# Differential attention: split scores, combination by a ratio, norm spread over the heads, on one Trainium2 core

## The chip, the cores and the metric

The kernel runs on one core of a Trainium2 chip. The metric is the device time of one execution in microseconds (us), lower is better. The kernel before took 3026.08 us, the median of three runs from 3018.17 to 3027.29 us.

## What is computed

Two transformer blocks over 512 tokens of width 1024 in float32; the change touches one sublayer of the second, the differential attention:

```
q, k, v = split(h @ w_qkv, 3)                 # 8 heads, two halves of 64 each in q and k, v of 128
q, k = rope on the first 16 of each 64;  q = q * 64 ** -0.5
p = softmax(q k^T)                            # for each head and each half c = 0, 1
a = p[:, :, 0] - lam_full * p[:, :, 1]
o = a @ v
o = rms_norm(o, subln_g) * (1 - lam_init)     # over the 128 of a head
return o.reshape(b, s, d) @ w_o
```

## The kernel before

The five engines are written out by hand: each has one list of instructions in program order (the blocks `sync`, `gpsimd`, `scalar`, `vector` and `tensor`), and they meet only through counting semaphores. An instruction that waits holds everything behind it on its engine. SP loads the weights (512 KB a unit) into four slots of `stage`. For every weight unit ScalarE writes a rounded copy `w_hi` (`hi`, L611), VectorE the remainder `w_lo` (`lo`, L1030), in rings of two; TensorE takes three products of half-width float32 (fp32r) for one of float32: hi by hi, lo by hi, hi by lo (`product`, L1706 to L1708), 24 matmuls a unit of 128 output columns.

The stage `qkv` has 24 such units: v in the first 8, then k, then q. VectorE copies each result out of PSUM into `raw` (L1612). For k and q, POOL issues four small DMAs that swap rows into `turned_raw` (L593), and one unit later VectorE turns the tile by three operations (L1620, L1622, L1626) into `k_t` or `q_t`. TensorE waits for all 16 tiles (`roped`, 48) before the first score.

The heads are 32 tiles m, four query tiles of 128 tokens to each of 8 heads. A tile passes: scores of both halves, 64 rows each, in float32 (L2269, TensorE, PSUM banks 0 to 3 in two pairs); maxima (L1641, VectorE); two exponentials with their sums (L984, ScalarE); reciprocal, scaling of half 1, combination (L1647, L1649, L1652, VectorE); four transposes (L2278, TensorE); copy into `PT` (L993, ScalarE); product with v (L2257, TensorE). The exponentials have two buffers, `E`. A finished head is copied to `o_raw` (`take_o`, L1634).

Only when all heads are done does the norm of o begin: squares (L1000), their sums by one-column matmuls (L2288), one root (L1002), reciprocal, then per head a broadcast copy `rexp` (L1665), its transposes (L2296), the scaling (L1672), the rounded copy `h_hi` (L1006) and the remainder `h_lo` (L1678). TensorE waits for the last `h_lo`, and then takes the 8 units of `w_o` (`attn_out`), L1706 to L1708 again, each followed by the addition to x.

## Time and profile before

| | us |
|---|---|
| three runs: lowest, median, highest | 3018.17, 3026.08, 3027.29 |
| profiled execution: its own time | 3019.3 |
| its span, first to last instruction | 3017.6 |
| mean granted TensorE clock | 0.964 of full |

Times in the rows count from the start of the span. PE is TensorE's matmuls, PEld its weight loads, DVE VectorE, ACT ScalarE, POOL GpSimd. A float32 matmul stands as two records, an fp32r one as one. The stretch in question runs from the last qkv unit, which ends at 2455.7 (its copy out of PSUM starts at 2455.74), to the start of the third unit of `w_o` at 2596.7.

### The profile page before, as it was taken

To read this page: it belongs to the slowest core of one execution; us is meant where nothing else is said; L and a number is where in the kernel's file an instruction comes from. 1 tells how busy PE (TensorE), PEld (TensorE's weight loads), DVE (VectorE), ACT (ScalarE), POOL (GpSimd) and SP (SyncE) were. 2 spreads that over 40 slices of the span, in tenths; PEclk is the share of its full clock that TensorE was granted. 3 is DMA by queue.
4 is the path that set the end of the run, shared out by engine and by line. 5 is a ranking of instruction groups with operands and counts; after the bars stand their busy time and mean duration, and the time that the engine had idled before them with its cause. 6 is when DMAs were issued, how large, how long until landed. Compare 5 with 4: busy or idle time off the path is not lost.

```text
span 3017.6 us, 40643 instructions
## 1 busy us (share of the span) xinstructions
PE 2874.0 (95%) x16133; PEld 2300.3 (76%) x16133; DVE 1456.7 (48%) x2079; ACT 977.1 (32%) x1548; POOL 233.1 (8%) x310
## 2 busy tenths in 40 slices
PE   7989978899999999999979999999999989899998
PEld 6844767788888787888868888788887854788887
DVE  4355655366677655555463332333323478433322
ACT  3234234333333223222233222322223236332222
POOL 1000010011100011001110000100001120100000
PEclk9769989999999999999979999999999999899999
DMA  5100500066322364555412223222232220122232
GB/s 216 69 1 1 180 24 3 3 219 227 116 94 96 113 201 153 195 195 190 149 53 91 97 93 93 87 98 97 96 96 95 97 71 1 56 91 97 96 91 71
DMA packets 91955, 310.20 MB, mean 103 GB/s; under 512 B 11824, under 2 KB 15664, under 8 KB 91696
## 3 DMA queue, kind: packets, MB, share of 16 engines
q1 hardware_dynamic: 69040, 231.77, 22.8%
q0 software_dynamic: 22784, 76.56, 7.6%
q8 instruction: 97, 1.59, 0.2%
q14 instruction: 34, 0.28, 0.0%
HBM read 305.14 MB, written 2.10 MB: 102 GB/s over the span
## 4 chain that ended last, share of the span: by engine, by line
PE 88%; DVE 7%; ACT 2%; issue 1%; DMA 0%; POOL 0%; SPq 0%; DVEq 0%; ACTq 0%
PE psum L1706 24%; PE psum L1708 24%; PE psum L1707 24%; PE psum L1931 1%; PE psum L1919 1%; PE psum L1871 1%; PE psum L1721 1%; PE psum L1781 1%; DVE nmax L1641 1%; PE psum L1777 1%; PE psum L1778 1%; PE psum L2269 1%; PE psum L2037 1%; PE psum L2092 1%; PE psum L1943 1%
## 5 line engine op out<-in xcount | busy, mean ns | idle before, releaser
L1030 DVE TENSOR_TENSOR w_lo<-stage,w_hi 128x1024 fp32r<-128x1024 f32 (+3 forms) x445 | 519.6, 1168 | 849.0 <-ACT w_hi L611 846.8
L1706 PE MATMUL psum<-h_hi,w_hi 128*128 128x512 f32 x2248 | 882.5, 393 | 12.2 <-POOL h_lo L578 8.3
L1707 PE MATMUL psum<-h_lo,w_hi 128*128 128x512 f32 x2248 | 879.4, 391 | 0.0
L1708 PE MATMUL psum<-h_hi,w_lo 128*128 128x512 f32 x2248 | 879.3, 391 | 0.0
L611 ACT ACTIVATE w_hi<-stage 128x1024 fp32r<-128x1024 f32 (+3 forms) x445 | 450.3, 1012 | 1267.8 <-PE psum L1708 1237.0
L1706 PEld LDWEIGHTS psum<-h_hi,w_hi 128*128 128x128 f32 x2248 | 424.1, 189 | 105.1 <-POOL h_lo L578 8.7
L1708 PEld LDWEIGHTS psum<-h_hi,w_lo 128*128 128x128 f32 x2248 | 424.0, 189 | 90.1
L1707 PEld LDWEIGHTS psum<-h_lo,w_hi 128*128 128x128 f32 x2248 | 424.2, 189 | 87.9
L1706 PE MATMUL psum<-hid_hi,w_hi 128*128 128x512 f32 x880 | 343.0, 390 | 6.5 <-DVE hid L1115 6.5
L1707 PE MATMUL psum<-hid_lo,w_hi 128*128 128x512 f32 x880 | 342.4, 389 | 0.0
L1708 PE MATMUL psum<-hid_hi,w_lo 128*128 128x512 f32 x880 | 342.4, 389 | 0.0
L1706 PEld LDWEIGHTS psum<-hid_hi,w_hi 128*128 128x128 f32 x880 | 165.2, 188 | 42.7 <-DVE hid L1115 8.7
L1707 PEld LDWEIGHTS psum<-hid_lo,w_hi 128*128 128x128 f32 x880 | 165.2, 188 | 34.4
L1708 PEld LDWEIGHTS psum<-hid_hi,w_lo 128*128 128x128 f32 x880 | 165.2, 188 | 34.3
L1115 DVE TENSOR_TENSOR hid<-s_buf,psum 128x512 f32<-128x512 f32 x88 | 60.5, 688 | 266.5 <-PE psum L1708 264.8
L1066 DVE CUSTOM_DVE_ANT_0 mod_w<-mod_w,c_act 128x1024 f32<-128x1024 f32 x144 | 175.6, 1219 | 0.0
L498 POOL DMA_DIRECT2D mod_w<-in_mod_w x144 | 76.9, 534 | 1125.7 <-DVE modv L1066 948.4
L668 ACT ACTIVATE hid_hi<-hid 128x512 f32 (+1 forms) x110 | 67.9, 618 | 56.0 <-DVE hid L1115 56.0
L622 ACT ACTIVATE norm_t<-xT 128x512 f32<-128x512 f32 x64 | 40.3, 630 | 131.9 <-DVE xT L1139 121.6
L519 POOL TENSOR_TENSOR rexp<-norm_t 128x512 f32<-128x512 f32 x7 | 9.0, 1286 | 945.2 <-ACT norm_t L622 945.2
L1122 DVE TENSOR_TENSOR hid_lo<-hid,hid_hi 128x512 f32 (+1 forms) x110 | 75.3, 685 | 0.0
L519 POOL TENSOR_TENSOR rexp<-rexp,norm_t 128x512 f32<-128x512 f32 x35 | 45.1, 1288 | 268.4 <-ACT norm_t L622 268.4
(397 smaller groups left out, 2744.8 us busy)
## 6 DMA issues: line engine op xcount, KB each, us to landing
stage<-in_up SPq DMA_DIRECT2D x220, 512.0 KB, 3.2
mod_w<-in_mod_w POOLq DMA_DIRECT2D x144, 512.0 KB, 4.1
stage<-in_down SPq DMA_DIRECT2D x80, 448.0 KB, 3.3
stage<-in_down SPq DMA_DIRECT2D x40, 512.0 KB, 3.5
stage<-in_w_in SPq DMA_DIRECT2D x24, 512.0 KB, 4.3
stage<-in_w_qkv SPq DMA_DIRECT2D x24, 512.0 KB, 3.2
stage<-in_w_merge SPq DMA_DIRECT2D x16, 512.0 KB, 4.5
PTn<-in_cmp_w SPq DMA_DIRECT2D x1, 4096.0 KB, 12.0
```

The costliest lines, as they stand in the source:

```text
L498: pool.dma_start(mod_w[:, slot], A["mod_w"][bass.ds(t, 1)].rearrange("a p n -> (a p) n")).then_inc(mod_in[slot], 16)
L519: pool.tensor_tensor(sq_sum, sq(n_norm, 0) if k == 1 else sq_sum, sq(n_norm, k), ALU.add).then_inc(acc_done, 1)
L611: act.activation(w_hi[:, c % 2, 0:kt * cols], stage[:, c % NSTAGE, 0:kt * cols], ACT.Copy).then_inc(hi_done, 1)
L622: act.activation(sq(n_norm, k), xT[:, k], ACT.Square).then_inc(sq_done, 1)
L668: act.activation(hid_hi[:, bass.ds(2 * i + q, 1), :].rearrange("p a n -> p (a n)"), hid[:, q], ACT.Copy).then_inc(hidhi_done, 1)
L1030: dve.tensor_tensor(w_lo[:, c % 2, 0:kt * cols], stage[:, c % NSTAGE, 0:kt * cols], w_hi[:, c % 2, 0:kt * cols].bitcast(F32), ALU.subtract ...
L1066: dve.tensor_tensor_reduce(out=mod_w[:, t % 2], in0=mod_w[:, t % 2], in1=c_act[:], scale=1.0, scalar=0.0, op0=ALU.mult, op1=ALU.add, accum ...
L1115: dve.tensor_tensor(hid[:, q], s_buf[:, q], taps[:, 1] if f == 0 else bank(s.tile + 2 * q + 1), ALU.mult).then_inc(hid_done, 1)
L1122: dve.tensor_tensor(hid_lo[:, tile, :].rearrange("p a n -> p (a n)"), hid[:, q], hid_hi[:, tile, :].rearrange("p a n -> p (a n)").bitcast( ...
L1706: pe.matmul(dst, wh[:, n], a_hi[:, k], start=start and n == 0, stop=False)
L1707: pe.matmul(dst, wh[:, n], a_lo[:, k], start=False, stop=False)
L1708: m = pe.matmul(dst, wl[:, n], a_hi[:, k], start=False, stop=stop and n == kt - 1)
```

## The change

1. k and q are split like weights: ScalarE rounds the turned tile (`qk_round`), VectorE writes the remainder (`qk_low`), and a score is three fp32r products per half (`score`) in place of one float32 product. Scores of a head wait for its own tiles, the first one for `raw_done`; the turning of the last two q tiles and three remainders are moved behind the first maxima, with the `lo` of the second unit of `w_o`.
2. Combination by a ratio: the scaling of half 1 over 512 columns goes; a ratio of one column is formed, and half 0 takes half 1 times the ratio. The common factor that is left goes into the norm, whose eps is multiplied by the square of the sum of half 0 (`var_o`).
3. `E` gets a third buffer; the transposes lag three tiles and use one bank; ScalarE copies the turned tile to `PT` ahead of the exponentials of its tile. `E` lies in `mod_w` and `c_act`, `o_raw` in `v_tok`, and `rope`, `raw`, `turned_raw` in `PT`.
4. Square, sum and variance of a head are moved between the tiles (`SQUARE_AT`, `SUM_AT`, `VAR_AT`). The root is taken in two parts; the spread is a matmul of `orstd` (no `rexp`), and the first two units of `w_o` are taken part by part as the heads get ready (`first_out`). POOL writes `h_lo` of the odd heads.

The core of the diff; "..." marks what is left out, the removed lines of the old functions for the most part:

```diff
+def by_token(x):
+    return x.rearrange("p (t n) -> p t n", t=TT)
+ROOTS = ((0, 5), (5, 8))
+SQUARE_AT = {4 * h + 12: h for h in range(6)}
+SUM_AT = {4 * h + 13: h for h in range(6)}
+VAR_AT = {4 * h + 14: h for h in range(5)}
...
-        q_t, k_t, v_tok, rope, raw, E, PT, o_raw, turned_raw = phase(
-            ("q_t", [P, KD, S], F32), ("k_t", [P, KD, S], F32), ("v_tok", [P, TT, D], F32), ("rope", [P, 2, S], F32),
-            ("raw", [P, 2, S], F32), ("E", [P, 2, 2, S], F32), ("PT", [P, 2, TT, S], F32), ("o_raw", [P, DIFF_HEADS, S], F32),
-            ("turned_raw", [P, 2, S], F32))
+        qk_hi, qk_lo, v_tok, PT, es, ovar = phase(
+            ("qk_hi", [P, 2 * KD, S], F32R), ("qk_lo", [P, 2 * KD, S], F32R), ("v_tok", [P, TT, D], F32),
+            ("PT", [P, 2, TT, S], F32), ("es", [P, DIFF_HEADS * TT, 2], F32), ("ovar", [P, DIFF_HEADS * TT], F32))
+        rope, raw, turned_raw = PT[:, 0, 0:2], PT[:, 1, 0:2], PT[:, 1, 2:4]
+        k_hi, q_hi, k_lo, q_lo = qk_hi[:, 0:KD], qk_hi[:, KD:], qk_lo[:, 0:KD], qk_lo[:, KD:]
+        spare = c_act[:].rearrange("p (a s) -> p a s", a=2)
+        E = [mod_w[:, n].rearrange("p (c s) -> p c s", c=2) for n in range(2)] + [spare]
+        o_sq = [norm_t[:, h % 2] for h in range(6)] + [spare[:, 0], spare[:, 1]]
+        o_raw = [v_tok[:, :, h * P:(h + 1) * P] for h in range(DIFF_HEADS)]
...
+for h in range(1, DIFF_HEADS, 2):
+    pool.wait_ge(ohi_done, h + 1)
+    pool.tensor_tensor(h_lo[:, h], turn_t[h % 4], h_hi[:, h].bitcast(F32), ALU.subtract).then_inc(olo_pool, 1)
...
+    def qk_round(m):
+        act.wait_ge(roped, 3 * (m - 7))
+        act.activation(qk_hi[:, m - 8], norm_t[:, m % 2], ACT.Copy).then_inc(qkhi_done, 1)
+    for n in range(23):
         hi(s.first + n + 2)
...
+        if n >= 10:
+            qk_round(n - 2)
...
+    def root_o(n):
+        first, last = ROOTS[n]
+        act.wait_ge(ovar_done, last)
+        act.activation(ostd[:, TT * first:TT * last], ovar[:, TT * first:TT * last], ACT.Sqrt,
+                       scale=float(D // P)).then_inc(ostd_done, 1)
+    def round_o(h):
+        act.wait_ge(ot_done, h + 1)
+        act.activation(h_hi[:, h], turn_t[h % 4], ACT.Copy).then_inc(ohi_done, 1)
...
+    for m in range(4 * DIFF_HEADS + 3):
+        if m >= 3:
+            g = m - 3
             h, j = g // 4, g % 4
             act.wait_ge(a_turned, g + 1)
+            if g == 0:
+                act.wait_ge(roped, 48)
             if h >= 2 and j == 0:
                 act.wait_ge(pv_done, h - 1)
             act.activation(PT[:, h % 2, :, j * P:(j + 1) * P],
-                           psum[:, 4 + g % 2, :].rearrange("p (t n) -> p t n", t=TT),
+                           psum[:, 4, :].rearrange("p (t n) -> p t n", t=TT),
                            ACT.Copy).then_inc(pt_done, 1)
...
+        if m < 4 * DIFF_HEADS:
+            act.wait_ge(max_done, m + 1)
+            for c in range(2):
+                act.activation(E[m % 3][:, c], psum[:, 2 - 2 * (m % 2) + c, :], ACT.Exp,
+                               bias=nmax[:, m % 2, c:c + 1],
+                               accum_out=es[:, m, c:c + 1]).then_inc(exp_done, 1)
+        if m == 0:
+            hi(s.first + 25)
+        if m < 3:
+            qk_round(21 + m)
+        if m in SQUARE_AT:
+            square_o(SQUARE_AT[m])
+    for step, h in (("sq", 6), ("root", 0), ("sq", 7), ("hi", 0), ("hi", 1), ("root", 1), ("hi", 2), ("hi", 3),
+                    ("hi", 4), ("hi", 5), ("hi", 6), ("hi", 7)):
+        {"sq": square_o, "hi": round_o, "root": root_o}[step](h)
...
+    def qk_low(m):
+        dve.wait_ge(qkhi_done, m - 7)
+        dve.tensor_tensor(qk_lo[:, m - 8], norm_t[:, m % 2], qk_hi[:, m - 8].bitcast(F32),
+                          ALU.subtract).then_inc(qklo_done, 1)
...
+    for n in range(24):
+        dve.wait_ge(unit_done, s.first + n + 1)
+        if n >= 10:
+            dve.wait_ge(roped, 3 * (n - 9))
+        dve.tensor_copy(raw[:, n % 2], bank(s.tile + n)).then_inc(raw_done, 1)
+        if n == 23:
+            continue
+        lo(s.first + n + 2)
+        if n >= 10:
+            qk_low(n - 2)
         if n >= 9:
+            turn_qk(n - 1)
...
+    def var_o(h):
+        cols = slice(TT * h, TT * h + TT)
+        dve.wait_ge(exp_done, 2 * TT * (h + 1))
+        dve.scalar_tensor_tensor(out=ovar[:, cols], in0=es[:, cols, 0], scalar=EPS * P / D, in1=es[:, cols, 0],
+                                 op0=ALU.mult, op1=ALU.mult).then_inc(ovar_step, 1)
+        dve.wait_ge(ovar_step, h + 1)
+        dve.wait_ge(ossq_done, h + 1)
+        dve.tensor_tensor(ovar[:, cols], ovar[:, cols], psum[:, 5, cols], ALU.add).then_inc(ovar_done, 1)
+    def rec_o(n):
+        cols = slice(TT * ROOTS[n][0], TT * ROOTS[n][1])
+        dve.wait_ge(ostd_done, n + 1)
+        dve.reciprocal(orstd[:, cols], ostd[:, cols]).then_inc(orstd_done, 1)
+    def norm_o(h):
+        if h >= 4:
+            if h % 2:
+                dve.wait_ge(olo_pool, h // 2 - 1)
+            else:
+                dve.wait_ge(olo_done, h // 2 - 1)
+        dve.wait_ge(obc_done, h + 1)
+        dve.scalar_tensor_tensor(out=by_token(turn_t[h % 4]), in0=o_raw[h], scalar=sub_gain[:, 0:1],
+                                 in1=by_token(psum[:, 3 * (h % 2), :]), op0=ALU.mult, op1=ALU.mult).then_inc(ot_done, 1)
+    def low_o(h):
+        dve.wait_ge(ohi_done, h + 1)
+        dve.tensor_tensor(h_lo[:, h], turn_t[h % 4], h_hi[:, h].bitcast(F32), ALU.subtract).then_inc(olo_done, 1)
...
-            dve.tensor_reduce(nmax[:, m % 2], psum[:, 2 * (m % 2):2 * (m % 2) + 2, :], AX.X, ALU.max,
+            dve.tensor_reduce(nmax[:, m % 2], psum[:, 2 - 2 * (m % 2):4 - 2 * (m % 2), :], AX.X, ALU.max,
                               negate=True).then_inc(max_done, 1)
+        if m == 0:
+            lo(s.first + 25)
+            qk_low(21)
         if 1 <= m <= M:
             g = m - 1
             b = g % 2
             dve.wait_ge(exp_done, 2 * g + 2)
-            dve.reciprocal(coef[:, b], esum[:, b]).then_inc(comb_step, 1)
-            dve.wait_ge(comb_step, steps + 1)
-            dve.tensor_scalar(E[:, b, 1], E[:, b, 1], coef[:, b, 1:2], neg_lam[:, 0:1], ALU.mult,
+            dve.reciprocal(coef[:, b, 1:2], es[:, g, 1:2]).then_inc(comb_step, 1)
+            dve.wait_ge(comb_step, 3 * g + 1)
+            dve.tensor_scalar(coef[:, b, 0:1], es[:, g, 0:1], coef[:, b, 1:2], neg_lam[:, 0:1], ALU.mult,
                               ALU.mult).then_inc(comb_step, 1)
...
+            dve.wait_ge(comb_step, 3 * g + 2)
+            dve.scalar_tensor_tensor(out=E[g % 3][:, 0], in0=E[g % 3][:, 1], scalar=coef[:, b, 0:1],
+                                     in1=E[g % 3][:, 0], op0=ALU.mult, op1=ALU.add).then_inc(comb_step, 1)
+        if 2 <= m <= 3:
+            qk_low(20 + m)
+        if 1 <= m <= 2:
+            turn_qk(21 + m)
+        if m >= 11 and (m - 11) % 4 == 0:
+            take_o((m - 11) // 4)
+        if m in VAR_AT:
+            var_o(VAR_AT[m])
+    for step, h in (("var", 5), ("take", 6), ("rec", 0), ("take", 7), ("norm", 0), ("var", 6), ("norm", 1), ("low", 0),
+                    ("var", 7), ("norm", 2), ("rec", 1), ("norm", 3), ("low", 2), ("norm", 4), ("low", 4),
+                    ("norm", 5), ("norm", 6), ("low", 6), ("norm", 7)):
+        {"take": take_o, "rec": rec_o, "norm": norm_o, "var": var_o, "low": low_o}[step](h)
...
+    def score(m):
+        h, cols = m // 4, slice(m % 4 * P, m % 4 * P + P)
+        pe.wait_ge(qklo_done, 9 + h)
+        if m == 0:
+            pe.wait_ge(raw_done, 23)
+        if m == 1:
+            pe.wait_ge(raw_done, 24)
+        for n, (q, k) in enumerate(((q_hi, k_hi), (q_lo, k_hi), (q_hi, k_lo))):
+            for c in range(2):
+                rows = slice(HD * c, HD * c + HD)
+                last = pe.matmul(psum[:, 2 - 2 * (m % 2) + c, :], q[rows, h, cols], k[rows, h, :],
+                                 start=n == 0, stop=n == 2)
+        last.then_inc(score_done, 1)
...
+    def sum_o(h):
         pe.wait_ge(osq_done, h + 1)
+        if h >= 1:
+            pe.wait_ge(ovar_done, h)
         for tt in range(TT):
+            last = pe.matmul(psum[:, 5, TT * h + tt:TT * h + tt + 1], o_sq[h][:, tt * P:(tt + 1) * P],
                              means[:, 0:1], start=True, stop=True)
         last.then_inc(ossq_done, 1)
...
+    def spread_o(h):
+        pe.wait_ge(orstd_done, 1 if h < ROOTS[0][1] else 2)
         if h >= 2:
             pe.wait_ge(ot_done, h - 1)
         for tt in range(TT):
+            at = TT * h + tt
+            last = pe.matmul(psum[:, 3 * (h % 2), tt * P:(tt + 1) * P],
+                             orstd[:, at:at + 1].to_broadcast([P, P]), ident, start=True, stop=True)
         last.then_inc(obc_done, 1)
+    def first_out(k):
+        s = seg["attn_out"]
+        kt, cols = shape_of(s.first)
+        pe.wait_ge(ohi_done, k + 1)
+        for e in range(2):
+            c = s.first + e
+            if k == 0:
+                pe.wait_ge(lo_done, c + 1)
+            wh, wl, dst = slot(w_hi, c, kt, cols, 2), slot(w_lo, c, kt, cols, 2), bank(s.tile + e)
+            pe.matmul(dst, wh[:, k], h_hi[:, k], start=k == 0, stop=False)
+            pe.matmul(dst, wl[:, k], h_hi[:, k], start=False, stop=False)
+            if k % 2:
+                pe.wait_ge(olo_pool, k // 2 + 1)
+            else:
+                pe.wait_ge(olo_done, k // 2 + 1)
+            last = pe.matmul(dst, wh[:, k], h_lo[:, k], start=False, stop=k == KD - 1)
+            if k == KD - 1:
+                last.then_inc(unit_done, 1)
...
+    for m in range(M + 3):
+        if m < M:
+            if m >= 2:
+                pe.wait_ge(exp_done, 2 * (m - 1))
+            score(m)
+        if m >= 3:
+            g = m - 3
+            pe.wait_ge(comb_step, 3 * (g + 1))
+            if g >= 1:
+                pe.wait_ge(pt_done, g)
+            for kt in range(TT):
+                last = pe.transpose(psum[:, 4, kt * P:(kt + 1) * P],
+                                    E[g % 3][:, 0, kt * P:(kt + 1) * P], ident)
+            last.then_inc(a_turned, 1)
+        if m >= 7:
+            weigh((m - 7) // 4, (m - 7) % 4)
+        if m in SUM_AT:
+            sum_o(SUM_AT[m])
+    for kt in range(TT):
+        weigh(DIFF_HEADS - 1, kt)
+    for step, h in (("sum", 6), ("spread", 0), ("spread", 1), ("sum", 7), ("out", 0), ("spread", 2), ("out", 1),
+                    ("spread", 3), ("out", 2), ("spread", 4), ("out", 3), ("spread", 5), ("out", 4),
+                    ("spread", 6), ("out", 5), ("spread", 7), ("out", 6), ("out", 7)):
+        {"sum": sum_o, "spread": spread_o, "out": first_out}[step](h)
+    def out_unit(n):
+        if n >= 2:
+            product(seg["attn_out"].first + n, 0, range(KD), (h_hi, h_lo), seg["attn_out"].tile + n, True, True)
+    mixed_out("attn_out", 7, out_unit)
```

VectorE (DVE), from the last copy out of PSUM to the first combination. Before:

```order
L1612 COPY raw<-psum 128x512 [waits roped,unit_done]
L1030 TENSOR_TENSOR w_lo<-stage,w_hi 128x1024 [waits hi_done]
L1620 SCALAR_TENSOR_TENSOR q_t<-turned_raw,rope 128x512 [waits raw_done,swapped0]
L1622 SCALAR_TENSOR_TENSOR raw<-raw,rope 128x512
L1626 TENSOR_TENSOR q_t<-q_t,raw 128x512 [waits roped]
L1620 SCALAR_TENSOR_TENSOR q_t<-turned_raw,rope 128x512 [waits raw_done,swapped1]
...
L1641 TENSOR_REDUCE nmax<-psum 128x2 [waits score_done] x2
L1647 RECIPROCAL coef<-esum 128x2 [waits exp_done]
L1649 TENSOR_SCALAR E<-E,coef,neg_lam 128x512 [waits comb_step]
L1652 SCALAR_TENSOR_TENSOR E<-E,coef 128x512 [waits comb_step]
```

Now (`PT` stands for `raw`, `mod_w` for `E`):

```order
L1672 COPY PT<-psum 128x512 [waits roped,unit_done]
L1720 TENSOR_REDUCE nmax<-psum 128x2 [waits score_done]
L1072 TENSOR_TENSOR w_lo<-stage,w_hi 128x1024 [waits hi_done]
L1651 TENSOR_TENSOR qk_lo<-norm_t,qk_hi 128x512 [waits qkhi_done]
L1720 TENSOR_REDUCE nmax<-psum 128x2 [waits score_done]
L1729 RECIPROCAL coef<-es 128x1 [waits exp_done]
L1731 TENSOR_SCALAR coef<-es,coef,neg_lam 128x1 [waits comb_step]
L1734 SCALAR_TENSOR_TENSOR mod_w<-mod_w,coef 128x512 [waits comb_step]
L1661 SCALAR_TENSOR_TENSOR norm_t<-PT 128x512 [waits raw_done,swapped0,qklo_done]
L1663 SCALAR_TENSOR_TENSOR PT<-PT 128x512
L1666 TENSOR_TENSOR norm_t<-norm_t,PT 128x512 [waits roped]
```

The maxima of tile 0 stand ahead of the second `w_o` remainder, and the turnings come after combinations.

TensorE, from the last product with v to the first products with `w_o`. Before (of eight groups of sums and eight of transposes one each is shown):

```order
L2257 MATMUL psum<-PT,v_tok 128x512 x3
L2288 MATMUL psum<-cst,norm_t 128x1 [waits osq_done]
L2288 MATMUL psum<-cst,norm_t 128x1 x3
...
L2296 MATMUL psum<-cst,rexp 128x128 [waits ot_done,orexp_done]
L2296 MATMUL psum<-cst,rexp 128x128 x3
L1706 MATMUL psum<-h_hi,w_hi 128x512 [waits lo_done,olo_done]
```

Now:

```order
L2338 MATMUL psum<-PT,v_tok 128x512 x3
L2348 MATMUL psum<-cst,c_act 128x1 [waits ovar_done,osq_done]
...
L2358 MATMUL psum<-cst,orstd 128x128 [waits orstd_done]
...
L2371 MATMUL psum<-h_hi,w_hi 128x512 [waits lo_done,ohi_done]
L2372 MATMUL psum<-h_hi,w_lo 128x512
L2377 MATMUL psum<-h_lo,w_hi 128x512 [waits olo_done]
...
L2358 MATMUL psum<-cst,orstd 128x128 [waits ot_done,orstd_done]
L2358 MATMUL psum<-cst,orstd 128x128 x3
L2371 MATMUL psum<-h_hi,w_hi 128x512 [waits ohi_done]
```

Two groups of sums are left there, and products with `w_o` stand between the spreads.

## Rows read from the trace of the kernel before

**Rows 1.** The page, part 4: chain that ended last, shares by engine.
```profile
PE 88%; DVE 7%; ACT 2%; issue 1%; DMA 0%; POOL 0%; SPq 0%; DVEq 0%; ACTq 0%
```

**Rows 2.** Windows: stretch, length, busy by engine, then granted clock (PEclk), DMA share, GB/s.
```profile
170.00:205.00 35.00, 32.91 (x73) 16.06 (x74) 16.33 (x45) 12.74 (x49) 0.00 (x0) 0.50 0.00 0
2457.85:2468.09 10.24, 3.78 (x8) 1.19 (x8) 6.00 (x9) 1.38 (x4) 0.84 (x2) 0.50 0.17 57
2468.09:2482.00 13.91, 9.51 (x42) 3.90 (x42) 13.51 (x23) 9.95 (x27) 0.00 (x0) 1.00 0.01 2
2482.00:2552.00 70.00, 64.84 (x251) 24.92 (x250) 67.31 (x108) 48.88 (x128) 0.00 (x0) 1.00 0.00 1
2563.66:2587.56 23.90, 17.56 (x65) 13.82 (x65) 13.48 (x25) 7.96 (x13) 0.00 (x0) 0.50 0.00 1
```

**Rows 3.** Timeline, VectorE, last qkv unit to fifth maxima: start, length, engine.
```profile
2455.74 0.69 DVE L1612 COPY raw<-psum 128x512 f32<-128x512 f32 x1 [1.13 <-PE psum L1708]
...
2461.55 0.69 DVE L1620 SCALAR_TENSOR_TENSOR q_t<-turned_raw,rope 128x512 f32<-128x512 f32 x1 [1.51 <-DMA turned_raw<-raw]
...
2465.75 1.23 DVE L1641 TENSOR_REDUCE nmax<-psum 128x2 f32<-128x1024 f32 x1 [2.18 <-PE psum L2269]
...
2475.19 1.22 DVE L1641 TENSOR_REDUCE nmax<-psum 128x2 f32<-128x1024 f32 x1
```

**Rows 4.** Timeline, one head in the steady stretch, VectorE.
```profile
2504.83 0.69 DVE L1634 COPY o_raw<-psum 128x512 f32<-128x512 f32 x1
2505.43 1.22 DVE L1641 TENSOR_REDUCE nmax<-psum 128x2 f32<-128x1024 f32 x1
2506.76 0.55 DVE L1649 TENSOR_SCALAR E<-E,coef,neg_lam 128x512 f32<-128x512 f32 x1
2507.34 0.75 DVE L1652 SCALAR_TENSOR_TENSOR E<-E,coef 128x512 f32<-128x512 f32 x1
2508.01 1.22 DVE L1641 TENSOR_REDUCE nmax<-psum 128x2 f32<-128x1024 f32 x1
...
2515.93 0.68 DVE L1634 COPY o_raw<-psum 128x512 f32<-128x512 f32 x1
```

**Rows 5.** The same stretch, TensorE and ScalarE.
```profile
2503.97 1.13 PE L2269 MATMUL psum<-k_t,q_t 64*128 64x512 f32 x4
2505.03 0.66 PE L2278 MATMUL psum<-cst,E 128*128 128x128 f32 x4
2505.52 1.02 PE L2257 MATMUL psum<-PT,v_tok 128*128 128x512 f32 x2
2506.48 1.13 PE L2269 MATMUL psum<-k_t,q_t 64*128 64x512 f32 x4
...
2504.85 0.59 ACT L993 ACTIVATE PT<-psum 128x512 f32<-128x512 f32 x1
```

**Rows 6.** Timeline from the last maxima to the third unit of w_o.
```profile
2549.82 1.22 DVE L1641 TENSOR_REDUCE nmax<-psum 128x2 f32<-128x1024 f32 x1
...
2559.01 9.57 PE L2288 MATMUL psum<-cst,norm_t 128*128 128x1 f32 x64
2565.91 1.28 ACT L1002 ACT_TABLE_LOAD   x1
2583.58 0.79 PE L1706 MATMUL psum<-h_hi,w_hi 128*128 128x512 f32 x1 [2.38 <-DVE h_lo L1678]
2596.74 1.06 ACT L611 ACTIVATE w_hi<-stage 128x1024 fp32r<-128x1024 f32 x1 [1.79 <-PE psum L1708]
...
2597.84 1.23 DVE L1030 TENSOR_TENSOR w_lo<-stage,w_hi 128x1024 fp32r<-128x1024 f32 x1 [3.55 <-ACT w_hi L611]
2602.18 1.06 ACT L611 ACTIVATE w_hi<-stage 128x1024 fp32r<-128x1024 f32 x1 [1.79 <-PE psum L1708]
```

**Rows 7.** Timeline, the next norm: spread by matmuls, and a remainder on POOL.
```profile
2632.63 1.16 PE L1742 MATMUL psum<-cst,rstd 128*128 128x128 f32 x8
...
2636.73 1.28 POOL L526 TENSOR_TENSOR h_lo<-norm_t,h_hi 128x512 fp32r<-128x512 f32 x1 [7.78 <-ACT h_hi L649]
```

141 lines of the change are left out of this document (28 added, 113 removed).

## The prediction

> **What bounds the kernel now.** I read the chain of waits first: TensorE holds 88% of it [rows 1], nearly all in weight products that the change leaves alone. A gain can only come from the stretch between the last qkv unit and the third unit of w_o, 2455.7 to 2596.7, 141.0 us. The windows show three different limits in it. At the start TensorE is busy 3.8 of 10.2 us, at half clock. In the heads VectorE is busy 67.3 of 70 us and TensorE 64.8, so both are nearly full; ScalarE, 48.9, is not. In the norm behind the heads TensorE works 17.6 of 23.9 us at half clock, again with gaps [rows 2]. The timeline gives the pace. A head lasts from one copy of o at 2504.83 to the next at 2515.93, 11.1 us for four tiles. A tile costs VectorE 1.33 us for the maxima and the reciprocal, 0.58 for the scaling and 0.67 for the combination, 2.58 in all, and 0.60 per head for the copy: 10.9 of the 11.1 [rows 4]. So VectorE sets the pace of the heads, and TensorE with 1.06 us of scores and 1.45 of transposes and product with v, 2.51 a tile, 10.0 a head, stands right behind it [rows 5].
>
> **The change part by part**, in three pieces; T is 2455.7.
>
> *Start.* Before, the first maxima come at T + 10.05 and the fifth at T + 19.5, after a DMA wait for the last swapped tile [rows 3]. Now TensorE scores tile 0 at T. VectorE's list, with the pitches of the rows: copy 0.6, then the scores are there; maxima 0 end at T + 2.3; two exponentials (0.68 apart and 0.78) to 3.8; ScalarE's `hi` 1.06 [rows 6]; `lo` 1.14 to T + 6.0; first remainder 0.6, to 6.6. This `hi` behind the exponentials makes VectorE stand 2.5 us. Tile 1 costs maxima 1.13, combination 1.05 and a turning of three operations of 0.69, some 1.9: 10.7. Tile 2 the same with a remainder, 4.7: 15.4. Tile 3 without a turning 2.8: the fifth maxima come at T + 18.1. **Gain 1.4 us.** Each edit that takes TensorE's wait away puts work in front of VectorE, so little of the 7.9 us idle is won. The swap of the last tile, which before was turned at T + 5.85 [rows 3], is hidden now, since its turning comes up at T + 13. The rounding (0.63) and the remainder (0.69) of the other tiles are hidden by a qkv unit of 24 matmuls, 5.44 us (from `hi` to `hi` at 2596.74 and 2602.18, [rows 6]): VectorE needs about 4.9 of it. POOL's DMAs and SP's loads keep their order and slack.
>
> *Heads.* VectorE: the scaling over 512 columns (0.58) becomes an operation of one column. I take 0.19, the pitch of the reciprocal, as its price (bounds 0.1 and 0.25). A tile costs 1.13 + 0.19 + 0.19 + 0.67 = 2.18, a head 8.7 plus the copy 0.6 plus two small operations of `var_o`, 0.4: 9.7 us. TensorE: the score is the uncertain price. A float32 score is four records in 1.13 us where a product with v has two in 1.02 [rows 5]. The two halves of 64 rows thus run side by side: two passes of 0.43 and some 0.2 us to fill and to change over make the 1.06. An fp32r matmul of 128 rows takes 5.44 / 24 = 0.227 us. Three pairs side by side are 0.68, with the 0.2 it is 0.88; the bounds are 0.68 without that and 1.36 + 0.2 where the halves do not overlap. I take 0.88, since the nearest row is the float32 pair of the same shape. With 1.45 unchanged a tile costs 2.33, four 9.3. A head's sums by one-column matmuls, 8 records, add 0.9 (64 records take 9.57 us partly at half clock, [rows 6]; the full-clock part is 0.11 apart): 10.2 us. So TensorE becomes the bound. Laid out in order it also stands 0.5 us before each sum, because the square waits behind the exponentials on ScalarE and VectorE's next maxima wait for the score behind it: 10.7 us a head. The seven tiles before the first sum go at VectorE's 2.18: 15.3 us. Then 5 heads of 10.7: 53.4. Fifth to last maxima is 68.7, against 2549.82 - 2475.19 = 74.6 [rows 3, 6]. **Gain 5.9 us.** The third `E` and the copy to `PT` ahead of the exponentials are worth nothing of their own in this sum: they let TensorE run three tiles behind, so that it no longer waits for the combination, and that wait is inside the 11.1.
>
> *Norm and first units.* Before, from the last maxima at 2549.82 to the third unit at 2596.7: 46.9 us. Of it 9.2 until the last product with v, 24.6 to the first product with w_o at 2583.58, 13.1 for two units [rows 6]. Now TensorE owes more behind the last maxima, because it lags: eight products with v (6.9), three groups of transposes (1.2), a sum (1.0), waits 1.1: 10.2. Then sum 6, two spreads of 0.9 each (8 records in 1.16 us with the drain, [rows 7]), a wait of 0.5 for the variance, sum 7: 4.1. Then 48 matmuls with w_o, 10.9, six spreads, 5.4, and waits of 2.6: half of these is POOL's last remainder, 1.28 us [rows 7], which comes behind ScalarE's last rounding and which the last matmuls wait for. Together 18.9. At the end both units free their slots at the same time, so `hi` 1.06 and `lo` 1.23 [rows 6] are in the open, less 0.4 of overlap: 1.9. Sum 35.1. **Gain 11.8 us.** The squares and roots of six heads are gone from the path; the two units of w_o fill the gaps of the rest.
>
> The table load for the root lasts 1.28 us in the row, and no idle stands before it [rows 6]; it lies here behind square 6, and the sum above carries it with 1.28. The Trainium skill, "ScalarE: Activation LUTs", section "What ACT_TABLE_LOAD costs", adds a drain of 1380 ns to each switch. By that rule the spreads would start about half a microsecond later and the gain would be 18.6, not 19.1; the row speaks for 1.28.
>
> *Clock.* The sum so far, 1.4 + 5.9 + 11.8 = 19.1, holds at full clock. TensorE goes to half clock at 2457.85, after it went idle, and comes back at 2468.09, after two float32 scores in a row; after that it stays at full clock though it is busy 9.5 of 13.9 us [rows 2]. Now its work at the start is thin: three scores in the first 9 us, then one tile in 3 to 5 us. It will fall at the same place and I expect it back only when the tiles come densely, at about T + 26. Until T + 22 half clock costs next to nothing, because VectorE sets the pace; until T + 26 it is 1.9 us, until T + 36 it is 7.5, since the products with v double there. In the norm a half-clock piece of 4 us would cost 2.7; I count a quarter of that, 0.7. **Together a gain of 16.5 us.** The profiled execution took 3019.3 us, so it would be 3002.8. The three runs before spread over 9 us, with the median 6.8 above the profiled execution. I set the result from the middle of the two, 3022.7: **3006 us**.
>
> **Rivals.**
> 1. *The halves do not overlap in fp32r.* Then a score is 1.56 us, a tile 3.0, a head 12.7 with its sums and waits. The heads take 82 us instead of 68.7, the gain of 19.1 shrinks to 5.2, and with the clock to 3: 3020. For it: no fp32r matmul of 64 rows stands in the trace. Against it: the float32 ones overlap [rows 5]. The Trainium skill, "TensorEngine Tiling (Array Packing)", section "Key Properties", has tiles run in parallel whatever the type; no row shows it for fp32r. Chance 0.09.
> 2. *Slower: TensorE stays at half clock through the heads.* At 170 to 205 TensorE ran scores, transposes and products with v of the first block at half clock for 35 us, busy 32.9 of them [rows 2], before the clock rose, so dense work of this kind does not lift it at once. Here the doubled work is 20 us a head against 10.7. Half clock until T + 46 takes 12 us off the gain, until T + 56 17.5, until the end of the heads 31: 12 us slower than before, 3035. The turning point is T + 59, some 30 us into the dense part. Against it: before, two scores sufficed at 2468, and the scores here fill both halves of the array. Chance 0.06.
> 3. *VectorE or the small operations cost more.* Each wait between two small operations is priced at 0.03 us; with 0.1 more on each of three a tile, and half clock until T + 36, the gain is 19.1 - 4.5 - 7.5 = 7: 3016. Chance 0.15.
> 4. *Better than laid out.* Score 0.68, clock back by T + 22 and no loss in the norm: the gain is 20.3, from the lower run of before (3018.2) 2998. If also the waits at the sums vanish, 2 to 3 us more. Chance 0.15, as the upper part of the forecast's own range.
>
> The forecast, a gain between 10 and 20, has 0.55 without number 4.
>
> **How the numbers follow.** About 0.3%, 9 us, is what a measurement of this kernel can tell from no change. The forecast and number 4 lie beyond it, 0.70, with a small edge of number 3: faster 0.72. Within: 1 and the rest of 3, 0.22. Slower: 2, 0.06. The range goes from 2993 (number 4 with its further 3 us, from the lower run) to 3019 (number 3, from the median); it leaves out number 2 and most of number 1.
>
> **What would show it.** Right: fifth maxima 18 us after the last qkv unit; 10.7 us between copies of o; four operations of VectorE a tile with no 512-column scaling; six score records of 0.23 pitch in pairs, some 0.9 us a tile; w_o's first matmul 14 us after the last maxima, its third unit 35 after them; low granted clock from T + 2 to T + 26 and little behind. Wrong: score records one after the other (1), granted clock 0.50 beyond T + 40 (2), VectorE idle less than 0.5 us a head with a pace of 11 (3), or a qkv unit longer than 5.44 us, which would mean that the split of q and k is not hidden.

## The result, and the profile after

| | before | after |
|---|---|---|
| median of the runs, us | 3024.0 (7 runs, 3018.2 to 3027.3) | 3004.2 (7 runs, 2996.8 to 3009.5) |
| ratio, 95% interval | | 0.9934 [0.9919, 0.9949] |
| profiled execution: its own time, its span, us | 3019.3, 3017.6 | 3000.8, 2998.9 |
| T, the end of the last qkv unit | 2455.7 | 2453.7 |
| fifth maxima | T + 19.5 | T + 18.3 |
| fifth to last maxima | 74.6 | 69.8 |
| last maxima to the third unit of w_o | 46.9 | 35.9 |
| T to the third unit of w_o | 141.0 | 124.0 |

The change is faster by 0.66%, the forecast said 3006 against a base of 3022.7. Later the same two kernels ran again in rounds of their own: 3003.4 against 3018.0, a ratio of 0.9948 [0.9935, 0.9961]. The gain is thus 15 to 20 us. In the two profiled executions 17.0 us lie between T and the third unit of w_o. The spans differ by 18.7: T comes 2.0 us earlier, and 0.3 us are lost again behind the third unit. Before T the change adds only the rounding and the remainder of k and q, and a qkv unit lasts 5.44 us in both kernels. The changed kernel and its variants are all alike up to T, and yet T lies anywhere from 2451.3 to 2459.1 in their traces; these 2.0 us thus cannot be put down to the change. So single runs are compared below by pieces counted from T, not by their whole time.

The shares of the chain of waits, on the page after, are as before to a point ([rows 1]):

```profile
PE 88%; DVE 7%; ACT 3%; issue 1%; POOL 0%; DMA 0%; SPq 0%; DVEq 0%; ACTq 0%
```

The windows after, for the stretch of half clock at the start, the heads, and the end (as [rows 2]: length, busy by engine with instructions in brackets, then the granted clock):

```profile
2459.87:2476.97 17.10, 10.33 (x39) 6.12 (x40) 16.67 (x30) 9.91 (x25) 0.00 (x0) 0.50 0.09 32
2477.00:2541.00 64.00, 62.09 (x335) 33.53 (x335) 59.21 (x113) 50.84 (x128) 0.00 (x0) 1.00 0.00 1
2541.00:2577.70 36.70, 31.92 (x175) 23.02 (x171) 17.06 (x35) 14.36 (x28) 5.12 (x4) 1.00 0.00 1
```

Three things are to be seen. The half clock (1.2 in place of 2.4 GHz) lasts from T + 6.2 to T + 23.3, and VectorE is busy 16.7 of these 17.1 us: it sets the pace there, not the slow TensorE. In the heads TensorE is now the fuller engine, 62.1 of 64 us, and VectorE is at 59.2, where it had 67.3 of 70. The end runs at full clock throughout, where before 23.9 us of it ran at half.

The start on VectorE after (timeline: start, length, engine, line; in brackets the idle time and what ended it), which answers to [rows 3]:

```profile
2454.61 1.23 DVE L1720 TENSOR_REDUCE nmax<-psum 128x2 f32<-128x1024 f32 x1 [0.20 <-PE psum L2328]
2458.29 1.23 DVE L1072 TENSOR_TENSOR w_lo<-stage,w_hi 128x1024 fp32r<-128x1024 f32 x1 [2.46 <-ACT w_hi L633]
2460.04 1.22 DVE L1720 TENSOR_REDUCE nmax<-psum 128x2 f32<-128x1024 f32 x1
...
2472.00 1.22 DVE L1720 TENSOR_REDUCE nmax<-psum 128x2 f32<-128x1024 f32 x1
```

The first maxima now come at T + 0.9 in place of T + 10, but VectorE then stands 2.46 us for `hi`, and the fifth maxima are only 1.2 us earlier than before.

One part of a head after, TensorE, then VectorE, from the copy of o on; these answer to [rows 4, 5]:

```profile
2502.29 0.50 PE L2328 MATMUL psum<-qk_hi 64*128 64x512 f32 x2
2502.63 0.40 PE L2328 MATMUL psum<-qk_hi,qk_lo 64*128 64x512 f32 x2
...
2503.18 0.66 PE L2392 MATMUL psum<-cst,c_act 128*128 128x128 f32 x4
2503.68 1.02 PE L2338 MATMUL psum<-PT,v_tok 128*128 128x512 f32 x2
2505.03 1.05 PE L2348 MATMUL psum<-cst,norm_t 128*128 128x1 f32 x8 [0.33 <-ACT norm_t L1010]
...
2501.16 0.68 DVE L1685 COPY v_tok<-psum 128x512 f32<-128x512 f32 x1
2501.76 1.21 DVE L1720 TENSOR_REDUCE nmax<-psum 128x2 f32<-128x1024 f32 x1
2503.08 0.27 DVE L1731 TENSOR_SCALAR coef<-es,coef,neg_lam 128x1 f32<-128x1 f32 x1
2503.39 0.75 DVE L1734 SCALAR_TENSOR_TENSOR mod_w<-mod_w,coef 128x512 f32<-128x512 f32 x1
2504.06 1.22 DVE L1720 TENSOR_REDUCE nmax<-psum 128x2 f32<-128x1024 f32 x1
2507.01 1.22 DVE L1720 TENSOR_REDUCE nmax<-psum 128x2 f32<-128x1024 f32 x1 [0.57 <-PE psum L2328]
```

A score is three pairs, from 2502.29 to the transposes at 2503.18: 0.89 us (laid out: 0.88). The operation of one column takes 0.31 to the next start, where 0.19 was laid out, so a tile costs VectorE 2.30 us (2504.06 - 2501.76), not 2.18. A head takes 10.74 us. In each head TensorE stands before the sum of squares: from the product with v to the sum it is 1.35 us (2503.68 to 2505.03), where without a wait it is 0.87 (e1, below), so 0.48 us are lost, 0.33 of them shown as idle. VectorE waits 0.57 us for the score behind the sum.

The end after, which answers to [rows 6]: TensorE, then ScalarE, then POOL:

```profile
2552.95 2.03 PE L2358 MATMUL psum<-cst,orstd 128*128 128x128 f32 x16
2556.17 0.48 PE L2371 MATMUL psum<-h_hi,w_hi 128*128 128x512 f32 x1
2562.41 0.50 PE L2377 MATMUL psum<-h_lo,w_hi 128*128 128x512 f32 x1 [0.97 <-DVE h_lo L1713]
2574.73 0.50 PE L2377 MATMUL psum<-h_lo,w_hi 128*128 128x512 f32 x1 [0.61 <-POOL h_lo L616]
2577.69 0.51 PE L1774 MATMUL psum<-h_hi,w_hi 128*128 128x512 f32 x1 [1.78 <-DVE w_lo L1072]
...
2549.55 0.63 ACT L1010 ACTIVATE c_act<-v_tok 128x512 f32<-128x512 f32 x1 [0.99 <-DVE v_tok L1685]
2550.19 1.28 ACT L1015 ACT_TABLE_LOAD   x1
2551.49 0.22 ACT L1015 ACTIVATE ostd<-ovar 128x20 f32<-128x20 f32 x1
...
2573.41 1.27 POOL L616 TENSOR_TENSOR h_lo<-rexp,h_hi 128x512 fp32r<-128x512 f32 x1 [3.74 <-ACT h_hi L1020]
```

The last maxima are at 2541.81, so the first product with w_o comes 14.4 us after them, and the third unit 35.9 us after them (laid out: 14.3 and 35.1). The two exposed waits that the prediction named are there: POOL's last remainder, and `hi` and `lo` of the third unit.

### The profile page after: what moved, and what is told of

Its sections match the earlier page's. It is cut to its first block, busy times and chain, and to the rows that moved or that the text cites. A ratio compares the mean times of both kernels' runs of the same rounds, so it can differ in the third digit from the quotient of the medians.

```text
span 2998.9 us, 40893 instructions
## 1 busy us (share of the span) xinstructions
PE 2863.0 (95%) x16229; PEld 2302.4 (77%) x16229; DVE 1454.5 (48%) x2100; ACT 986.1 (33%) x1565; POOL 238.2 (8%) x314
## 4 chain that ended last, share of the span: by engine, by line
PE 88%; DVE 7%; ACT 3%; issue 1%; POOL 0%; DMA 0%; SPq 0%; DVEq 0%; ACTq 0%
PE psum L1774 24%; PE psum L1775 24%; PE psum L1776 24%; PE psum L1999 1%; DVE nmax L1720 1%; PE psum L1987 1%; PE psum L1939 1%; PE psum L1849 1%; PE psum L1789 1%; PE psum L1845 1%; PE psum L1846 1%; PE psum L2105 1%; PE psum L2160 1%; PE psum L2011 1%; PE psum L2158 1%
## 5 line engine op out<-in xcount | busy, mean ns | idle before, releaser
L1774 PE MATMUL psum<-h_hi,w_hi 128*128 128x512 f32 (+1 forms) x2232 | 877.1, 393 | 11.6 <-POOL h_lo L597 8.3
L1775 PE MATMUL psum<-h_lo,w_hi 128*128 128x512 f32 (+1 forms) x2232 | 874.1, 392 | 0.0
L1776 PE MATMUL psum<-h_hi,w_lo 128*128 128x512 f32 (+1 forms) x2232 | 874.0, 392 | 0.0
L1774 PEld LDWEIGHTS psum<-h_hi,w_hi 128*128 128x128 f32 (+1 forms) x2232 | 421.1, 189 | 103.7 <-POOL h_lo L597 8.7
L1776 PEld LDWEIGHTS psum<-h_hi,w_lo 128*128 128x128 f32 (+1 forms) x2232 | 421.2, 189 | 88.8
L1775 PEld LDWEIGHTS psum<-h_lo,w_hi 128*128 128x128 f32 (+1 forms) x2232 | 421.3, 189 | 87.2
L1774 PEld LDWEIGHTS psum<-hid_hi,w_hi 128*128 128x128 f32 x880 | 165.6, 188 | 42.9 <-DVE hid L1157 8.7
L1776 PEld LDWEIGHTS psum<-hid_hi,w_lo 128*128 128x128 f32 x880 | 165.7, 188 | 34.4
L1775 PEld LDWEIGHTS psum<-hid_lo,w_hi 128*128 128x128 f32 x880 | 165.7, 188 | 34.4
```

The source lines that it names most:

```text
L1774: pe.matmul(dst, wh[:, n], a_hi[:, k], start=start and n == 0, stop=False)
L1775: pe.matmul(dst, wh[:, n], a_lo[:, k], start=False, stop=False)
L1776: m = pe.matmul(dst, wl[:, n], a_hi[:, k], start=False, stop=stop and n == kt - 1)
```

## The experiments

Each kernel but e9 and e12 changes one thing in the changed kernel. All stretches are from the trace of one execution; e11 is the changed kernel once more, and shows how well they repeat.

| run | its time | fifth maxima | a steady head | fifth to last | last maxima to third unit |
|---|---|---|---|---|---|
| before | 3019.3 | T + 19.5 | 11.09 | 74.6 | 46.9 |
| the change | 3000.8 | T + 18.3 | 10.74 | 69.8 | 35.9 |
| the change again, e11 | 3006.2 | T + 18.3 | 10.74 | 69.8 | 35.9 |
| e1, float32 score | 3004.7 | T + 18.5 | 10.91 | 71.1 | |
| e2, score by halves | 3005.1 | T + 18.4 | 10.76 | 70.8 | |
| e3, ratio undone | 3013.3 | T + 19.2 | 11.30 (two of 12.4) | 76.7 | |
| e4, units behind the norm | 3008.8 | T + 18.3 | 10.74 (one of 12.1) | 71.2 | 39.6 |
| e5, round first | 3002.4 | T + 15.9 | 10.74 | 69.8 | |
| e6, fillers | 3011.1 | T + 19.8 | 10.74 | 72.1 | |
| e7, sums later | 3001.2 | T + 18.3 | 10.15 | 67.7 | 36.0 |
| e8, norm behind the heads | 3012.9 | T + 18.3 | 9.80 | 66.0 | 49.9 |
| e10, fewer fillers | 3005.8 | T + 18.3 | 10.74 | 70.7 | |
| e12, sums later, float32 score | 3001.2 | T + 18.5 | 10.81 | 70.6 | |

The whole times mislead in one more way. In every variant but e4 and e9 the clock also fell to half for 3.4 us just behind the start of the third unit of w_o, outside these stretches; in e5 it made that unit 1.6 us longer than in the change. In both traces of the change it did not fall there.

### What paces the heads: e1, e7, e12, e3

**e1** gives the score back its float32 form:

```diff
-                    for n, (q, k) in enumerate(((q_hi, k_hi), (q_lo, k_hi), (q_hi, k_lo))):
-                        for c in range(2):
...
+                    for c in range(2):
+                        rows = slice(HD * c, HD * c + HD)
+                        last = pe.matmul(psum[:, 2 - 2 * (m % 2) + c, :], q_hi[rows, h, cols].bitcast(F32),
+                                         k_hi[rows, h, :].bitcast(F32), start=True, stop=True)
```

> The changed kernel with each score taken as one float32 product per half of the rounded q and k (the remainders are left out of the score, though still written), so that only TensorE's score changes. Theory (TensorE paces the heads at 10.74 us each: four tiles of 2.34, the sums 0.98, a wait of 0.33): a score costs 1.06 us again in place of 0.90, so a head takes 10.74 + 4 x 0.16 = 11.4 us, and the time from the fifth to the last maxima goes from 69.8 to about 74. Rival (VectorE paces them, as before the change): a head stays at 10.7 to 10.9 us and fifth to last maxima at 70 to 71 us. Nothing else moves.

TensorE's timeline in e1, from one score to the next; two tiles, the second with a sum:

```profile
2515.17 1.13 PE L2327 MATMUL psum<-qk_hi 64*128 64x512 f32 x4
2516.23 0.66 PE L2391 MATMUL psum<-cst,mod_w 128*128 128x128 f32 x4
2516.72 1.02 PE L2337 MATMUL psum<-PT,v_tok 128*128 128x512 f32 x2
2517.59 1.05 PE L2347 MATMUL psum<-cst,norm_t 128*128 128x1 f32 x8
2518.56 1.13 PE L2327 MATMUL psum<-qk_hi 64*128 64x512 f32 x4
```

The score costs 1.06 us again, 0.17 more, and a head takes 10.91: 0.17 more, not 0.66. By the letter of the expectation the rival had it, VectorE as the bound. But TensorE goes without a wait here: it is 0.87 us from the product with v to the sum. The changed kernel's 0.48 us before the sum are gone, taken up by the added work, and 0.66 less 0.48 is what shows. Two readings were left: TensorE's own work bounds the head, or VectorE's does and TensorE has room. The next two runs tell them apart.

**e7** moves the sums one tile, the variances two tiles later:

```diff
-SUM_AT = {4 * h + 13: h for h in range(6)}
-VAR_AT = {4 * h + 14: h for h in range(5)}
+SUM_AT = {4 * h + 14: h for h in range(6)}
+VAR_AT = {4 * h + 16: h for h in range(5)}
```

> The changed kernel with the sums of a head's squares one tile later on TensorE and the variance two tiles later on VectorE. Theory: TensorE's wait of 0.33 us for the square in each head goes, a head takes 10.4 us in place of 10.74, and fifth to last maxima 67.5 us in place of 69.8. Rival: another wait takes its place (the tile with the copy of o on VectorE), and a head stays at 10.7 us or more.

TensorE in e7, from a product with v to the score behind the sum:

```profile
2507.33 1.02 PE L2338 MATMUL psum<-PT,v_tok 128*128 128x512 f32 x2
2508.19 0.95 PE L2348 MATMUL psum<-cst,norm_t 128*128 128x1 f32 x8
2509.07 0.50 PE L2328 MATMUL psum<-qk_hi 64*128 64x512 f32 x2
```

The wait before the sum is gone, and the head falls by 0.59 us to 10.15, more than the 0.34 that was expected from the idle time alone: the wait measured by starts was 0.48. Both engines are now full: TensorE's four tiles of 2.34 and the sum's 0.88 less 0.09 of overlap are its 10.15, VectorE has 4 x 2.30 + 0.60 + 0.27 = 10.07. Fifth to last maxima fall by 2.1 us; 0.9 more would be there, but in e7 the half clock lasted longer (below).

**e12** puts the float32 score of e1 on top of e7.

> e7 and e1 together: the sums later, and the score as one float32 product per half of the rounded q and k (the remainders are left out of the score). In e1 the score's 0.66 us a head showed as 0.17 only. Theory (TensorE's own work is the bound at 10.15 to 10.25 us a head, and in e1 its wait of 0.48 us before the sum took up the rest): with that wait gone, as in e7, the whole 0.66 shows, a head takes 10.15 + 0.66 = 10.8 us. Rival (VectorE's 10.07 paces e7, TensorE has slack): a head takes 10.2 to 10.5 us.

TensorE and VectorE in e12:

```profile
2505.96 0.95 PE L2347 MATMUL psum<-cst,norm_t 128*128 128x1 f32 x8
2506.84 1.13 PE L2327 MATMUL psum<-qk_hi 64*128 64x512 f32 x4
...
2508.01 1.23 DVE L1720 TENSOR_REDUCE nmax<-psum 128x2 f32<-128x1024 f32 x1 [0.65 <-PE psum L2327]
```

A head takes 10.81: the whole 0.66 shows. So TensorE's work bounds the head, 10.15 us of it in the changed kernel, with a wait of 0.5 and 0.1 of lost overlap on top, and the split score is worth 0.17 us a head where that wait stands and 0.66 where it does not.

**e3** brings the scaling over 512 columns back. Both reciprocals are taken, and the first operation of `var_o` sets eps alone:

```diff
...
-                        dve.tensor_scalar(coef[:, b, 0:1], es[:, g, 0:1], coef[:, b, 1:2], neg_lam[:, 0:1], ALU.mult,
+                        dve.tensor_scalar(E[g % 3][:, 1], E[g % 3][:, 1], coef[:, b, 1:2], neg_lam[:, 0:1], ALU.mult,
...
```

> The changed kernel with the ratio undone: both reciprocals are taken, half 1 is scaled over 512 columns, half 0 takes it, and the variance gets eps alone. Only VectorE's work grows, by about 0.3 us a tile (0.6 in place of 0.31). Theory (VectorE at 10.2 us a head lies just under TensorE's 10.7): a head takes 4 x 2.6 + 0.6 + 0.3 = 11.4 us, and fifth to last maxima about 74 us. Rival (VectorE has slack of more than 1 us a head, since TensorE waits for it nowhere): a head stays at 10.7 to 10.9 us.

The two operations in e3, the window from its fifth to its twelfth maxima, and two windows in its heads:

```profile
2515.14 0.55 DVE L1731 TENSOR_SCALAR c_act<-c_act,coef,neg_lam 128x512 f32<-128x512 f32 x1
2515.72 0.75 DVE L1734 SCALAR_TENSOR_TENSOR c_act<-c_act,coef 128x512 f32<-128x512 f32 x1
...
2476.08:2494.10 18.02, 17.40 (x80) 8.85 (x78) 17.52 (x30) 13.06 (x35) 0.00 (x0) 0.81 0.00 0
2513.80:2517.00 3.20, 3.20 (x8) 1.64 (x10) 2.83 (x6) 1.95 (x6) 0.00 (x0) 0.50 0.00 0
2537.70:2541.00 3.30, 3.30 (x12) 1.58 (x10) 2.63 (x6) 1.93 (x5) 0.00 (x0) 0.50 0.00 0
```

The operation takes 0.58 us to the next start in place of 0.31, and a head 11.30 in place of 10.74. VectorE's own work is then 4 x 2.57 + 0.60 + 0.27 = 11.15, within 0.15 of the head, and it sets the pace. In two heads the clock fell to half for 3.4 us, as the windows show, with TensorE busy all through them; these heads took 12.4, 1.1 more. At the start the half clock lasted until T + 26.1, but it cost nothing here: the seven tiles from the fifth to the twelfth maxima took 18.04 us, which is VectorE's own 2.58 each (the window's clock, 0.81, is the mean of a part at half and a part at full). Without the two slow heads, fifth to last maxima would be 74.5 of the measured 76.7, 4.7 more than in the change: seven tiles of 0.27 and five heads of 0.56. So with the ratio taken back the heads last as long as before the change (74.6). The ratio is worth about all of the 4.8 us by which they became shorter, though the sums now lie in them; and the start loses 0.8 us without it too (T + 19.2).

### Whether the halves overlap: e2

```diff
-                    for n, (q, k) in enumerate(((q_hi, k_hi), (q_lo, k_hi), (q_hi, k_lo))):
-                        for c in range(2):
+                    for c in range(2):
+                        for n, (q, k) in enumerate(((q_hi, k_hi), (q_lo, k_hi), (q_hi, k_lo))):
```

> The changed kernel with the six products of a score in another order: all three of half 0, then all three of half 1, in place of turn and turn about. If two products lie beside each other only when they stand side by side in the program on different rows, the score takes 5 x 0.23 + 0.3, about 1.4 us in place of 0.90, a head 10.74 + 4 x 0.5 = 12.7 us, and fifth to last maxima about 84 us. If the order does not matter, a head stays at 10.74 us.

TensorE's score in e2; the records of the same operands stand together in a line:

```profile
2515.51 0.51 PE L2328 MATMUL psum<-qk_hi 64*128 64x512 f32 x2
2515.85 0.40 PE L2328 MATMUL psum<-qk_hi,qk_lo 64*128 64x512 f32 x2
2516.08 0.40 PE L2328 MATMUL psum<-qk_lo,qk_hi 64*128 64x512 f32 x2
2516.41 0.66 PE L2392 MATMUL psum<-cst,mod_w 128*128 128x128 f32 x4
```

The order does not matter: 0.90 us a score, 10.76 a head. The fp32r halves overlap, though in the program three products on the same rows stand in front of the first on the other rows. The two records of each line start 0.01 us apart. Rival 1 falls for good.

### The half clock at the start: e6, e10

e6 puts 40 products that nobody reads into TensorE's waits between the first scores. e10 puts in 24 (its expectation says 25); its edit:

```diff
+                        for _ in range({2: 4, 3: 9, 4: 5, 5: 1}.get(m, 0)):
+                            keep_busy([256])
                         if m >= 2:
                             pe.wait_ge(exp_done, 2 * (m - 1))
...
+                        if m == 4:
+                            keep_busy(5 * [256])
```

> The changed kernel with 40 products of 256 columns, read by nobody, put into TensorE's waits between the first five scores. If the idle waits are what lets the granted clock fall at T + 6, it stays whole through the start, and the fifth maxima come at T + 17 to T + 18.3, up to 1.3 us earlier than now; VectorE sets the order there, so most of the half clock is hidden and under 1 us is my value. Rival (the half clock costs the start the 1.9 us that the prediction gave it): the fifth maxima come at T + 16.4.

> As e6, with 25 products of 256 columns of 0.446 us each (as measured there), so that none lasts longer than the wait that it fills. The clock stays whole. If the half clock from T + 6 to T + 23 costs the start nothing, since VectorE works there without a wait for TensorE, the fifth maxima come at T + 18.3 as in the change; if it costs what the prediction gave it (1.9 us), at T + 16.4.

The fillers of e6 lasted longer than the waits: 19 of them took 8.47 us, 0.446 each, where the wait was 4.45 us. The fifth maxima came 1.5 us late, so e6 shows only that busy waits keep the clock whole. e10 has fewer. Its windows from T to the fifth maxima and behind them, and the fifth maxima at T + 18.3 (T is 2456.17):

```profile
2456.00:2479.00 23.00, 20.12 (x107) 13.79 (x106) 19.69 (x32) 12.37 (x30) 1.97 (x4) 1.00 0.09 27
2479.50:2482.90 3.40, 3.35 (x12) 2.08 (x12) 3.29 (x7) 2.55 (x7) 0.00 (x0) 0.50 0.00 0
...
2474.50 1.22 DVE L1720 TENSOR_REDUCE nmax<-psum 128x2 f32<-128x1024 f32 x1
```

At full clock up to there all five maxima stand where the change has them, within 0.02 us. So the half clock up to T + 18 costs nothing. From there to T + 23.3, where it ends in the change, it costs nothing either: the tiles keep VectorE's 2.30 up to the twelfth maxima at T + 34.4. It costs something only once the products with v have begun. In e2, e7 and e8 it lasted until T + 26.5, in e10 it fell for 3.4 us at T + 23.3: in all four the twelfth maxima come 0.9 to 1.0 us later than in the change. In e3 it lasted nearly as long, and cost nothing under VectorE's slower pace. In e4 it fell for 3.4 us in the middle of the heads, at T + 42.9, and that head took 12.11 us in place of 10.74.

### The start: e5

```diff
+                hi(s.first + 25)
                 for m in range(4 * DIFF_HEADS + 3):
...
-                    if m == 0:
-                        hi(s.first + 25)
...
                         lo(s.first + 25)
+                    if m == 1:
                         qk_low(21)
```

> The changed kernel with ScalarE's rounding of the second unit of w_o ahead of the first exponentials, where ScalarE stands idle, and the first remainder of a q tile behind the second maxima. Theory: VectorE's stand of 2.46 us before the remainder of w_o goes, the second maxima come at about T + 3.5 in place of T + 6.4, and the fifth at T + 15.9 in place of T + 18.3; fifth to last maxima stay at 69.8 us. Rival: the tiles behind are held by TensorE at half clock and by the turning, and the fifth maxima come at T + 17.5 to T + 18.3.

VectorE in e5 after T = 2456.03:

```profile
2456.97 1.22 DVE L1719 TENSOR_REDUCE nmax<-psum 128x2 f32<-128x1024 f32 x1 [0.20 <-PE psum L2328]
2458.11 1.22 DVE L1071 TENSOR_TENSOR w_lo<-stage,w_hi 128x1024 fp32r<-128x1024 f32 x1
2459.24 1.22 DVE L1719 TENSOR_REDUCE nmax<-psum 128x2 f32<-128x1024 f32 x1
```

The second maxima come at T + 3.2, the fifth at T + 15.9: 2.4 us won, the whole of the stand. The rounding took ScalarE's idle time. That the whole time did not fall (3002.4) is T, 2.4 us later in this execution, and the 1.6 us that the half clock costs in the third unit.

### The end: e4, e8

**e4** takes the first two units of w_o as ordinary units behind the last spread.

```diff
-                                ("spread", 3), ("out", 2), ("spread", 4), ("out", 3), ("spread", 5), ("out", 4),
...
-                    if n >= 2:
-                        product(seg["attn_out"].first + n, 0, range(KD), (h_hi, h_lo), seg["attn_out"].tile + n, True, True)
+                    if n == 0:
+                        pe.wait_ge(olo_done, 4)
+                        pe.wait_ge(olo_pool, 4)
+                    product(seg["attn_out"].first + n, 0, range(KD), (h_hi, h_lo), seg["attn_out"].tile + n, True, True)
```

> The changed kernel with the first two units of w_o taken as ordinary units behind the norm, in place of part by part between its spreads. Theory: the 48 products of 0.23 us (10.9 us) are hidden in the norm by the change; without it the norm's chain of spread, scaling, rounding and remainder ends only a few us earlier and the products follow, so the third unit starts about 42 to 45 us after the last maxima in place of 35.9, and the granted clock drops to half in the norm, as it did before. Rival: the gain of the end comes from the early sums and the spread by a product, and the interleaving gives less than 3 us: 36 to 39 us.

The first product with w_o in e4, and the windows of the first 14 products:

```profile
2571.90 0.77 PE L1774 MATMUL psum<-h_hi,w_hi 128*128 128x512 f32 x1 [4.04 <-issue]
...
2571.00:2577.90 6.90, 6.00 (x14) 4.83 (x15) 0.00 (x0) 0.00 (x0) 0.80 (x1) 0.51 0.00 0
```

The third unit starts 39.6 us after the last maxima, 3.7 later than in the change. TensorE stood idle for 4.04 us, and its clock fell to half 0.8 us before it started again; 14 products at 0.427 in place of 0.228 us are 2.8 of the 3.7. At full clock the interleaving itself would thus win about 1 us, since the gap of `hi` and `lo` before the third unit is gone in e4: on this one trace, its main gain is the clock. The expectation, 42 to 45, fell; the rival's 36 to 39 was nearer.

**e8** takes all squares, sums and variances behind the last head.

```diff
-SQUARE_AT = {4 * h + 12: h for h in range(6)}
-SUM_AT = {4 * h + 13: h for h in range(6)}
-VAR_AT = {4 * h + 14: h for h in range(5)}
+SQUARE_AT = {}
+SUM_AT = {}
+VAR_AT = {}
...
```

> The changed kernel with all squares, sums and variances behind the last head, as before the change, the rest of the norm as it is. Theory: TensorE loses 0.98 + 0.33 us a head, VectorE 0.3 us; a head takes 4 x 2.30 + 0.6 = 9.8 to 10.2 us, bounded by VectorE, fifth to last maxima 64 to 66 us (gain 4 to 5), while the last maxima to the third unit grow from 35.9 by six squares and sums of about 1 us each, to 41 to 43 us. In all 0 to 3 us slower than the change. Rival: the early sums are worth much more, over 5 us.

One of the sums behind the last head in e8:

```profile
2552.08 1.84 PE L2348 MATMUL psum<-cst,norm_t 128*128 128x1 f32 x8 [0.41 <-DVE ovar L1694]
```

The heads go at VectorE's 9.80 us and win 3.8 us in all. The end loses 14.0: five of the sums wait 0.41 us each for the variance before them, the clock falls to half for 13.6 us, and the root, which needs them all, comes behind. Net 10.2 us are lost, so the rival was right: more than 5 us hang on the early sums. But 14.0 is more than the 11.0 by which the change shortened the end. In e8 sums and variances take turns, where the kernel before took all 64 one-column products in one go. So e8 prices the early sums within the changed kernel, not against the kernel before. What the spread by a product is worth by itself was not tried.

### A version that beats both: e9

e9 has the edits of e5 and e7 and a new end. ScalarE takes the first root (five heads) behind the copy of tile 30, where it stands idle; TensorE takes spreads 0 and 1 and sum 6 between the last products with v, and the first part of w_o right behind them; the remainder of head 7 is VectorE's; the third unit takes its 16 products with `w_hi` before it waits for `w_lo`.

```diff
+                    if m == 4 * DIFF_HEADS + 1:
+                        root_o(0)
...
+                for step, h in (("weigh", 0), ("spread", 0), ("spread", 1), ("weigh", 1), ("sum", 6), ("weigh", 2), ("weigh", 3),
+                                ("out", 0), ("spread", 2), ("out", 1), ("spread", 3), ("sum", 7), ("out", 2), ("spread", 4),
...
+                        pe.wait_ge(hi_done, c + 1)
...
+                        for k in range(KD):
+                            pe.matmul(dst, wh[:, k], h_hi[:, k], start=k == 0, stop=False)
+                            pe.matmul(dst, wh[:, k], h_lo[:, k], start=False, stop=False)
+                        pe.wait_ge(lo_done, c + 1)
```

> The changed kernel with the rounding first (as e5), the sums later (as e7) and another end: the first root where ScalarE stands idle behind the last exponentials, spreads 0 and 1 between the last products with v, the first part of w_o right behind these products, the remainder of head 7 on VectorE, and the third unit of w_o with the products that need only its rounded copy first. Expected against the change: fifth maxima at T + 15.9 (gain 2.4), fifth to last maxima 67.7 us (gain 2.1), last maxima to third unit 30 us in place of 35.9 (TensorE's own work behind the last product with v: sums 1.9, spreads 4.9, products 11.7, near 18.5 us, with about 2 us of waits, behind the 10.3 us up to there), so some 10 us below the change, 2993 to 2996 us. Rival: the end is held by the chain of scaling, rounding and remainder from head to head at 2.3 us, and gains 3 us at most: 2997 to 3000 us.

> The changed kernel as it is, on the same chip and in the same rounds as the others, for a direct comparison: 3000 to 3006 us.

| five rounds, the same chip | median, us | against before |
|---|---|---|
| before (11 runs) | 3018.0 | |
| the change again, e11 (5 runs) | 3003.4 | 0.9948 [0.9935, 0.9961] |
| e9 (6 runs) | 2994.3 | 0.9921 [0.9906, 0.9935] |

In e9 the first root, its first product with w_o, and its third unit stand so:

```profile
2543.57 1.28 ACT L1015 ACT_TABLE_LOAD   x1
...
2551.63 0.79 PE L2373 MATMUL psum<-h_hi,w_hi 128*128 128x512 f32 x1
2571.63 0.50 PE L2418 MATMUL psum<-h_hi,w_hi 128*128 128x512 f32 x1 [0.50 <-ACT w_hi L633]
```

Fifth maxima T + 15.9 (2.4 won), fifth to last 66.7 (3.2 won), last maxima (2538.95) to third unit 32.7 (3.2 won): T to third unit is 115.2 us against 124.0, 8.8 won, and the medians differ by 9.1. The start came as expected. The heads won 1.1 more than expected: a head is 10.15 as in e7, but here the half clock ended at T + 19.6 and not at T + 26.5. The end won 3.2 of the 5.9 expected, as the rival's figure had it. That the whole time still lies in the expected range owes something to the heads. The miss at the end lies ahead of the first product with w_o: this comes 12.7 us after the last maxima, where the expectation had 10.3, because spreads 0 and 1 and sum 6, 2.6 us of work, were moved there and were priced as if they were free. From there to the third unit TensorE needs 20.0 us, close to the 20.5 expected, and 0.50 of these is the wait for the rounding of the third unit.

## Why the prediction came out as it did

- **Start**, laid out as a gain of 1.4, measured 1.2. Right in every step: the stand for `hi` 2.46 (2.5), the fifth maxima at T + 18.3 (18.1), the swap and the split of the tiles hidden, a qkv unit 5.44 us in both. e5 shows that the stand was the one thing between this gain and 3.6.
- **Heads**, 5.9 laid out, 4.8 measured. The pace, 10.7, was right (10.74), and so were its parts, TensorE's 10.2 and a wait of 0.5 before the sum, as e7 and e12 show. The score, 0.89, was right. The term that was mis-sized is VectorE's operation of one column: 0.31 us, beyond its upper bound of 0.25, which had been set from the reciprocal alone. It costs where VectorE paces: the seven tiles before the first sum took 16.1 us (2.30 each) in place of 15.3, which is 0.8 of the 1.1 us that the term missed. The other 0.3 lies in the 20 tiles behind, 53.7 in place of 53.4. What the third `E` and the early copy to `PT` are worth was not tried; that they add nothing of their own stays argued.
- **Norm and first units**, 11.8 laid out, 11.0 measured. To the first product 14.4 (14.3), to the end of the two units 19.6 (18.9), exposed `hi` and `lo` 1.9 (1.9). What was mis-sized is the waits in between, laid out as 2.6: counted by the starts of the products they take 3.0. There are four of them, shown as 0.97, 0.19, 0.18 and 0.61 of idle time, three for a remainder and one (0.18) for a rounded copy; the largest is for the remainder of head 2 on VectorE, where the prediction had half of the 2.6 for POOL's last one. The last 0.3 lies in the products and spreads, a little slower than laid out.
- **Clock**, a loss of 2.6 laid out, none measured. Both terms failed: at the start the clock came back 2.7 us sooner than laid out, and in the norm it never fell. The half clock was there, T + 6.2 to T + 23.3 where the prediction had until T + 26, and e10 shows that it costs nothing while VectorE is full; the 1.9 us stood for a stretch that it did not reach. That the size was not absurd is seen in e7 and e8, where it did reach T + 26.5 and took 0.9. In the norm it never fell, since the products with w_o keep TensorE busy; e4, where they do not, pays 2.8. The price was set high as well: 2.7 us for 4 us of half clock, where e3 and e4 show 1.1 to 1.4 for 3.4 us in the heads and 2.8 for 6.8 us at the end.
- **The sum.** 19.1 at full clock became 17.0, and the loss of 2.6 became none: the two errors of 2.1 and 2.6 us cancel, and 16.5 stood against 17.0. That the total came out so close is in part luck: of the cancelled errors, and of T, which differs by more than 2 us from one execution to the next.
- **The rivals.** Number 1 falls with the pairs in the trace and with e2; its sum was loose too, since heads of 82 us in place of 68.7 leave 5.8 of the 19.1, not 5.2. Number 2 did not come; e3 and e4 give its price, 1.1 to 1.4 us a head for 3.4 us of half clock, but no trace had half clock for longer in the heads. Number 3 came true in its first half, by one operation a tile. Number 4 had the clock right and the score wrong.
- **The page on table loads.** The table load lasts 1.28 us, begins 0.01 us after the square's end (2550.19 against 2549.55 + 0.63), and the root starts 0.02 us after it: no drain shows, as [rows 6] had it. The Trainium skill, "ScalarE: Activation LUTs", section "What ACT_TABLE_LOAD costs", adds 1380 ns to a switch; the trace differs, and the measurement decides. For parallel tiles the Trainium skill, "TensorEngine Tiling (Array Packing)", section "Key Properties", says that they run at once. It names no type, so "whatever the type" in the prediction was a reading of its silence; the traces agree for fp32r, 0.23 us a pair against 0.227 for one product of 128 rows [rows 6].

## What to carry to other kernels

A wait inside the busiest engine's list swallows what is added to its work and hides what an edit is worth: undo an edit alone and it looked worth 0.17 us a head, with the wait gone it was worth 0.66. Before an early piece of side work is placed, ask what the bound engine stands for in front of it; one tile later was worth 0.6 us a head here. In these runs a half clock cost time only where TensorE was the one that was waited for, and filling its gaps with real work (the first units of w_o) was worth more by the clock that it kept (2.8 us) than by the work that it hid (about 1). Before the cost of a slow stretch is taken out of a comparison, look at the pace inside it: in e3 the same stretch was free.

## What was not expected of the hardware

- Products on the other half of the rows start beside the first ones even when three products stand before them in the program: in e2 a score took 0.90 us, against 0.89 in the turn-about order.
- A VectorE operation of one column with two operands of one column as scalars takes 0.27 us, 0.31 to the next start, where a reciprocal of one column takes 0.15 and 0.19. What part of it each operand costs was not tried.
- A product of 256 columns in float32 took 0.446 us in e6, one of 512 columns 0.88 (five products with v in a row, 2547.76 to 2552.14): float32 costs by columns, and 3.9 times an fp32r product of 512 columns, 0.227.
- The clock fell to half for 3.4 us inside the heads in e3 and e4, with TensorE busy for the whole of these stretches and in other executions at other places or not at all; a difference of 1 to 1.5 us between two single executions can be this alone.
